# Modulation halves as products in column groups of TensorE, and second-block handovers without counters of free banks

## What is computed

```python
# first block
c_act = jax.nn.silu(c)
ada = c_act @ w_ada[l] + b_ada[l]                    # 1024 -> 6144
sh1, sc1, g1, sh2, sc2, g2 = jnp.split(ada, 6, axis=-1)
h = modulate(rmsnorm(x, norm1_g[l]), sh1, sc1)
z = h @ w_in[l]
# convolutions, RG-LRU, head norms, w_out, then a PEER expert layer
# second block
proj = rms_norm(x, w) @ w_in
# block attention on one half of the heads, gated delta rule on the other:
t_inv = lax.linalg.triangular_solve(a + eye, eye)    # 64 x 64 chunks
u = t_inv @ (v * beta); w = t_inv @ (k_beta * jnp.exp(gc))
# scan over chunks: v_new = u - w @ S; o = q @ S + intra @ v_new; S = S * g + k @ v_new
```

## Time and profile before

| | |
|---|---|
| runs | 1891.62, 1891.71, 1889.61 us (median 1891.62) |
| profiled execution | 1888.98 us, its span 1887.3 us |
| mean granted TensorE clock | 0.979 |
| TensorE busy | 1824.0 us, 97% |
| VectorE, ScalarE, GpSimd busy | 1522.8, 716.2, 1046.0 us |

### The profile page before, as it was taken

The page is one execution under the profiler, slowest core; times in us unless marked ns, Lnnn a source line. Parts: engine busy times, 40 slices in busy tenths (PEclk is TensorE's granted clock), DMA queues, the critical chain, the costliest instruction groups (busy, mean ns, idle before and its releaser), DMA issues.

```text
span 1887.3 us, 29394 instructions
## 1 busy us (share of the span) xinstructions
PE 1824.0 (97%) x10499; PEld 1599.6 (85%) x10499; DVE 1522.8 (81%) x2519; ACT 716.2 (38%) x1157; POOL 1046.0 (55%) x651
## 2 busy tenths in 40 slices
PE   8998999999999999999999999999999998999887
PEld 8877788999999999999988888888888685887666
DVE  7886888869999888888499999999998886655542
ACT  2333333333333444444333333333333434236652
POOL 1333236688888655556567767676775563345012
PEclk8998999999999999999999999999999999999999
DMA  8642343699999689988899999999997231210011
GB/s 312 215 159 81 117 138 108 206 316 317 327 321 323 227 310 312 309 308 303 314 360 359 360 357 359 355 362 356 366 356 254 72 96 60 79 45 3 2 67 46
DMA packets 159920, 440.52 MB, mean 233 GB/s; under 512 B 13648, under 2 KB 62928, under 8 KB 156752
## 3 DMA queue, kind: packets, MB, share of 16 engines
q1 hardware_dynamic: 64400, 254.71, 38.8%
q0 software_dynamic: 36864, 134.23, 18.9%
q10 hardware_dynamic: 58560, 50.34, 8.1%
HBM read 386.80 MB, written 52.43 MB: 233 GB/s over the span
## 4 chain that ended last, share of the span: by engine, by line
PE 85%; DVE 8%; ACT 2%; DMA 2%; issue 2%; ACTq 0%; SPq 0%; POOL 0%; DVEq 0%
PE PS L964 14%; PE PS L973 14%; PE PS L965 14%; PE PS L1263 9%; PE PS L1264 9%; PE PS L1272 9%; PE PS L1230 4%; PE PS L1308 2%; DVE arena L1948 2%; PE PS L991 1%; PE PS L1299 1%; PE PS L1004 1%; DVE arena L2093 1%; PE PS L999 1%; DMA xres<-in_x 1%
## 5 line engine op out<-in xcount | busy, mean ns | idle before, releaser
L852 POOL TENSOR_TENSOR w_lo<-raw,w_hi 128x1024 fp32r<-128x1024 f32 x299 | 720.2, 2410 | 727.6 <-ACT w_hi L1496 726.5
L1496 ACT ACTIVATE w_hi<-raw 128x1024 fp32r<-128x1024 f32 x332 | 351.7, 1060 | 924.2 <-PE PS L973 576.5
L964 PE MATMUL PS<-act_hi,w_hi 128*128 128x384 f32 (+1 forms) x1584 | 578.2, 365 | 6.9 <-ACT w_hi L1496 3.1
L965 PE MATMUL PS<-act_lo,w_hi 128*128 128x384 f32 (+1 forms) x1584 | 565.4, 357 | 0.0
L973 PE MATMUL PS<-act_hi,w_lo 128*128 128x384 f32 (+1 forms) x1584 | 338.6, 355 | 0.1
L964 PEld LDWEIGHTS PS<-act_hi,w_hi 128*128 128x128 f32 x1584 | 300.6, 190 | 44.1 <-issue 8.5
L965 PEld LDWEIGHTS PS<-act_lo,w_hi 128*128 128x128 f32 x1584 | 300.7, 190 | 22.2 <-issue 1.4
L973 PEld LDWEIGHTS PS<-act_hi,w_lo 128*128 128x128 f32 x1584 | 286.0, 189 | 23.8 <-issue 0.9
L1263 PE MATMUL PS<-w_hi,act_hi 128*128 128x512 f32 x768 | 299.9, 390 | 3.6 <-ACT arena L1649 3.6
L1264 PE MATMUL PS<-w_hi,act_lo 128*128 128x512 f32 x768 | 299.5, 390 | 0.0
L2317 DVE TENSOR_TENSOR act_lo<-arena,act_hi 128x384 fp32r<-128x384 f32 x128 | 249.0, 1945 | 28.6 <-ACT act_hi L1707 28.6
(11 more groups left out here) (352 smaller groups left out, 1979.6 us busy)
## 6 DMA issues: line engine op xcount, KB each, us to landing
raw<-in_expert_u SPq DMA_DIRECT2D x128, 512.0 KB, 5.9
raw<-in_expert_v SPq DMA_DIRECT2D x128, 512.0 KB, 6.4
raw<-in_w_in SPq DMA_DIRECT2D x52, 512.0 KB, 3.6
arena<-in_w_ada SPq DMA_DIRECT2D x24, 1024.0 KB, 6.8
gel_d<-arena ACTq DMA_DIRECT2D x64, 384.0 KB
gates_d<-arena ACTq DMA_DIRECT2D x12, 2048.0 KB, 15.8
arena<-gates_d SPq DMA_DIRECT2D x32, 768.0 KB, 6.9
arena<-gel_d SPq DMA_DIRECT2D x32, 768.0 KB, 8.7
```

Source lines behind the costliest of these rows:

```text
L852: pool.tensor_tensor(w_lo[:, k % SPLIT, :], raw[:, k % RAW, :], w_hi[:, k % SPLIT, :].bitcast(F32), ALU.subtract).then_inc(lo_split, 1)
L964: pe.matmul(own, w, act_hi[:, c, 0:n_tok], start=(i == 0), stop=False)
L965: pe.matmul(own, w, act_lo[:, c, 0:n_tok], start=False, stop=False)
L1496: act.activation(w_hi[:, k % SPLIT, :], raw[:, k % RAW, :], ACT.Copy).then_inc(hi_split, 1)
```

## The change

Halves 0 to 3 of the modulation are no longer summed over c on VectorE. c_tiles holds for each of the eight chunks 128 by 32 numbers, the first column cs, the others zero. ada_first(h) multiplies them with the pieces: for each of the two pieces four products of 512 columns, each into its own group of 32 partitions (and so of the array's columns) of one bank. VectorE copies that bank to acc (gathered), and ada_half sums over the partitions as before. Halves 2 and 3 have places of their own (ada_x), so their transfers wait for nothing. x comes in two parts ahead of half 0. The warm-up products go from 36 to 16. ada_first(2) stands before step 2 of the first pair and ada_first(3) before step 7. sum_ready and its waits and nops are gone; the roots wait for sq_used. bank_free is gone; wait_free waits for the counter that the reader raises anyway, and the readers' last operation raises it itself.

```diff
+        ada_x = region("ada_x", 6160, 4, 2048)
+        c_tiles = region("c_tiles", 28184, KC, 32)
...
+        def emptied(name):
+            kind, n, tb = name[0], name[1] if len(name) > 1 else 0, name[-1]
+            if kind in ("x", "xt") or (kind == "m" and n == 0):
+                return d_ready, TB + TB * n + tb + 1
+            if kind == "m":
+                return m1_ready, TB * (n - 1) + tb + 1
+            return {"ba": (ba_row, 1), "bat": (ba_sb, 1), "cum": (cum_in, 1),
+                    "gcr": (at_ready, n + 1), "br": (at_ready, n + 1), "kk": (at_ready, n + 1), "qk": (at_ready, n + 1),
+                    "kt": (tok_act, n + 1), "vt": (tok_dve, n + 1),
+                    "wt": (wu_ready, n + 1), "u": (wu_ready, n + 1), "ws": (vn_ready, n), "su": (state_ready, n + 1),
+                    "o": (o_ready, n + 1) if n < TB - 1 else (g_scaled, GH * TB),
+                    "av": (avt_ready, n + 1), "gt": (gn_done, n + 1)}[kind]
...
         def wait_free(eng, *name):
             n = JOBS[name]
             if n >= 4:
-                eng.wait_ge(bank_free[n % 4], sum(READERS[n % 4:n:4]))
+                eng.wait_ge(*emptied(NAMES[n - 4]))
...
             def ada_half(h):
-                for i in (2 * h, 2 * h + 1):
-                    if i >= 4:
-                        sp_.wait_ge(*piece_used(i - 4))
...
+                for half in range(2):
+                    piece, landed_in, _ = ada_piece(h, half)
+                    if h in (4, 5):
+                        sp_.wait_ge(ada_read, h - 3)
+                    elif h >= 6:
+                        sp_.wait_ge(ada_used, 2 * (h - 6) + half + 1)
+                    sp_.dma_start(piece, A["w_ada"][h][:, 2048 * half:2048 * half + 2048]).then_inc(landed_in, 16)
...
+            for i in range(2):
+                own = slice(4 * i, 4 * i + 4)
+                sp_.dma_start(xres[:, own, :], A["x"].rearrange("(c p) t -> p c t", p=P)[:, own, :]).then_inc(x_in[i], 16)
             ada_half(0)
-            sp_.dma_start(xres[:, :, :], A["x"].rearrange("(c p) t -> p c t", p=P)).then_inc(x_in, 16)
             ada_half(1)
...
                 mm.then_inc(sq_used, 1)
-                if c == count - 1:
-                    pe.wait_ge(sq_used, first + count)
-                    pe.nop().then_inc(sum_ready, 1)
...
+            def ada_first(h):
+                if h == 0:
+                    pe.wait_ge(c_ready, 2)
+                if h == 3:
+                    pe.wait_ge(ada_acc, 3)
+                for half in range(2):
+                    piece, landed_in, count = ada_piece(h, half)
+                    pe.wait_ge(landed_in, count)
+                    for g in range(4):
+                        mm = pe.matmul(PS[32 * g:32 * g + 32, ADA_BANK[h], :], c_tiles[:, 4 * half + g, :],
+                                       piece[:, 512 * g:512 * g + 512], start=(half == 0), stop=(half == 1),
+                                       skip_group_check=True)
+                mm.then_inc(ada_read, 1)
...
-            for n in range(36):
+            for n in range(16):
                 pe.matmul(PS[:, 7, 0:P], ones[:, :], ones[:, :], start=True, stop=True)
...
+            ada_first(0)
+            norm_back(1, 7)
+            ada_first(1)
             ada_half(0)
-            norm_back(1, 7)
             ada_half(1)
...
                 if i == 0:
-                    idle_products(12, 2)
+                    idle_products(12, 6)
+                if i == 2:
+                    ada_first(2)
+                if i == 7:
+                    ada_first(3)
...
-            weighted(0)
-            weighted(1)
+            def gathered(h):
+                dve.wait_ge(ada_read, h + 1)
+                if h >= 2:
+                    dve.wait_ge(ada_done, h - 1)
+                v.tensor_copy(acc[:, h % 2, :], PS[:, ADA_BANK[h], :]).then_inc(ada_acc, 1)
+            norm_invert(0)
+            gathered(0)
+            gathered(1)
...
-                    per_head(VB[:, tb % 2, :], ("vt", tb), beta, 4 * tb)
-                    chain.wait()
-                    freed(dve.nop(), "kt", tb)
-                    freed(dve.nop(), "vt", tb)
-                    dve.nop().then_inc(tok_dve, 1)
+                    per_head(VB[:, tb % 2, :], ("vt", tb), beta, 4 * tb, last=tok_dve)
...
-                        chain.post(v.tensor_tensor(d, d, PS[:, bank("x", n, tb), 0:256], ALU.subtract))
-                    chain.wait()
-                    if n < LEVELS - 1:
-                        freed(dve.nop(), "x", n, tb)
-                    freed(dve.nop(), "xt", n, tb)
-                    dve.nop().then_inc(d_ready, 1)
+                        v.tensor_tensor(d, d, PS[:, bank("x", n, tb), 0:256], ALU.subtract).then_inc(d_ready, 1)
```

More of the change, by code:

```diff
@@ L178, in _jobs @@
         if kind == "products":
-            job(("gcr", *n), 2)
+            job(("gcr", *n))
             job(("br", *n))
@@ L424, in build @@
         consts_in = sem("consts_in")
[L425 removed]
+        x_in = [sem(f"x_in{i}") for i in range(2)]
         ada_in = [sem(f"ada_in{i}") for i in range(4)]
+        ada_x_in = [sem(f"ada_x_in{i}") for i in range(2)]
         ada_used = sem("ada_used")
[L428 removed]
+        ada_read = sem("ada_read")
         ada_acc = sem("ada_acc")
@@ L564, in wait_free, with ada_piece @@
             if n >= 4:
-                eng.wait_ge(bank_free[n % 4], sum(READERS[n % 4:n:4]))
+                eng.wait_ge(*emptied(NAMES[n - 4]))
         def unit_bank(n):
             return n % 4 if n < 12 else n % 2 if n < 32 else (n + 1) % 2
[L571 to L575, removed]
+        def ada_piece(h, half):
+            if h in (2, 3):
+                return ada_x[:, 2 * (h - 2) + half, :], ada_x_in[h - 2], 32
+            n = 2 * (h % 2) + half
+            return ada_w[:, n, :], ada_in[n], 16 * (1 if h < 2 else (h - 4) // 2 + 2)
         def cvp(n):
@@ L1501, in square, with root @@
                 act.activation(sq[:, n % 2, :], src, ACT.Square).then_inc(sq_ready, 1)
-            def root(index, width):
-                act.wait_ge(sum_ready, index + 1)
+            def root(index, width, sums, summed):
+                act.wait_ge(sums, summed)
                 if index >= 2:
@@ L1939, in weighted @@
                     dve.wait_ge(ada_done, h - 1)
-                for c in (range(4 if h in PE_SHARE else KC) if part is None else range(4 * part, 4 * part + 4)):
-                    i = 2 * h + c // 4
+                for c in range(KC) if part is None else range(4 * part, 4 * part + 4):
+                    piece, landed_in, count = ada_piece(h, c // 4)
                     if c % 4 == 0:
-                        dve.wait_ge(ada_in[i % 4], 16 * (i // 4 + 1))
-                    w = ada_w[:, i % 4, 512 * (c % 4):512 * (c % 4) + 512]
+                        dve.wait_ge(landed_in, count)
+                    w = piece[:, 512 * (c % 4):512 * (c % 4) + 512]
                     if c == 0:
@@ L1963, in _ @@
             v.tensor_scalar(cs, cth, 0.5, None, ALU.mult).then_inc(c_ready, 1)
+            chain.link(v.memset(c_tiles[:, :, :], 0.0))
+            v.tensor_scalar(c_tiles[:, :, 0], cth, 0.5, None, ALU.mult).then_inc(c_ready, 1)
             dve.wait_ge(c_ready, 1)
@@ L2393, in per_head @@
                 for h in range(GH):
-                    chain.post(v.tensor_scalar(h4(dst)[:, h, :], PS[:, bank(*name), h * P:(h + 1) * P],
-                                               scalars[:, at + h:at + h + 1], second, *ops))
+                    ins = v.tensor_scalar(h4(dst)[:, h, :], PS[:, bank(*name), h * P:(h + 1) * P],
+                                          scalars[:, at + h:at + h + 1], second, *ops)
+                if last is not None:
+                    ins.then_inc(last, 1)
             def all_heads(ap):
@@ L2409, in _ @@
                         else:
-                            dve.wait_ge(pads_ready, 1)
+                            chain.wait()
                         v.tensor_tensor(cin[:, n % 2, 3:515], PS[:, unit_bank(n), :], rr, ALU.mult).then_inc(p_dve, 1)
```

169 lines of the change are left out of this document (48 added, 121 removed).

## The result

The changed kernel takes 1871.97 us (median of four runs, 1868.33 to 1875.54) where the kernel before took 1890.61 beside it: 0.9901 of its time, 95% interval [0.9886, 0.9915], 18.6 us less. Run twice more beside other kernels it gave 1874.36 and 1875.54 us, 0.9918 [0.9903, 0.9933] and 0.9918 [0.9902, 0.9934]. The profiled execution took 1873.56 us.

What follows compares the result with a forecast made beforehand. TensorE, busy for 97% of the span, was taken as the bound. Savings of 6.1 + 2.1 + 1.0 + 2.7 + 0.1 = 12.0 us gave a median of 1879.6 us against 1891.62, range 1876 to 1887.5.

Steps and rivals of the forecast that it cites:

- Start, -6.1: Kernel start: early x and halves on TensorE bring first normed 1.9, second 3.1 and the pair's end 1.1 us; 6.1 in all.
- a bound of 2 us on the clock: Uncertainty given to the whole sum for TensorE's clock: plus or minus 2 us.
- Sums, second block, -2.1: Second block: TensorE no longer waits for its own sum; four of eight stalls count, 0.53 us each, 2.1 us saved.
- Sums, first block, -1.0: First block: nine head and token sums have such a stall, most beside VectorE; 1.0 us saved.
- Handovers, -2.7: Chain from 1698 to 1786: some twelve handovers shorter by 0.1 to 0.3 us without counters and nops; 2.7 us saved.
- The bound that I set: Handover saving lies between nothing and the 3.9 us of issue in the chain 1752 to 1786 and the like before it.
- Two groups at a time: In ada_first only two column groups run together, 3.6 us per half; total -6.4 us, 1885.2 us; chance 0.24.
- One after the other: In ada_first the column groups run serially, 6.9 us per half; total +7.2 us, 1898.8 us, slower; chance 0.06.
- Lead lost: Start's gain vanishes through a 1.2 GHz clock or unchanged later times; only 5.9 us remain, 1885.7 us; chance 0.10.
- waits do not go: Stalls behind sums and readers' waits stay as long, so only the start counts; 1885.5 us; chance 0.05.
- 1.3 us for the halves: Uncertainty of the sum for ada_first at the start, if a half takes 1.7 us: -1.3 us.

Runs made afterwards that it cites:

- the part alone: Kernel before with only the new start: halves 0 to 3 in column groups, x in two parts ahead, 16 warm-up products; 0.9978, 4.2 us less.
- sums alone: Kernel before with only the counter of finished sums and its waits and nops removed; 0.9968 of the kernel before, 6.0 us less.
- the parts: Kernel before with one part each: new start, 4.2 us less; no counter of finished sums, 6.0; no counters of free banks, 6.6.
- the full-width products: Changed kernel with each of the 32 products of ada_first at full width, so none runs beside another; 1892.68 us, 1.0008 of the kernel before.
- the order of transfers alone: Kernel before with x in two parts ahead of half 0 and 16 warm-up products, all halves still on VectorE; 1.0012 of the kernel before.

## Why the prediction was right or wrong

**Start, -6.1.** The mechanism and its times are confirmed step by step: sums over at 18.76 (forecast 18.9), half 0 at 22.3 (22.9), first normed 28.68 (28.9), second 44.50 (44.5), the pair's end 5.7 us earlier (6.1). I had chosen 2.0 us per half from rows with two groups; it is 1.85. The scaled figure of the Trainium skill (TensorE: Matmul & The Clock Gate, Part 3), an estimate of 2.2 us, was on the high side: the ratio measured is 3.7, not 3.2. But this is the better of two starts. Of the seven profiled executions with this start three have the first normed at 28.7 to 29.0 and four at 31.1 to 31.8. In two other executions of the changed kernel the lead at the gates is 2.7 and 3.2 us. The third one's chain:

```profile
4.22 6.24 PE PS L1080 x32
10.46 11.30 PE PS L1011 x64
21.76 3.57 PE PS L1066 x16
25.33 1.05 PE PS L1019 x4
26.38 1.85 PE PS L1066 x16
```

The warm-up products take 6.24 and not 5.26 us (I had 4.8): TensorE passes 12 records per microsecond from 8 us on in the first and only from 10 us on in the third. Then the clock falls for the sums sooner, between 12 and 13 and not at 14 us, and they take 11.3 and not 9.3. With 16 warm-up products their end varies from 9.5 to 11.0 between executions, with 36 it was 14.7 to 15.3, beside x at 14.5. That the shorter warm-up brought this into play is argued from these times; no run changed it alone. My sum had it only as a bound of 2 us on the clock. So the forecast of this term was right for one outcome and some 3 us too good for the other; the part alone gave 4.2 us over eleven runs.

**Sums, second block, -2.1: too small.** The price per stall was right (0.50 for 0.53). Two steps failed. I counted four stalls of 0.53; by the chains of the two kernels five count, at 0.50, 0.47, 1.16, 0.52 and 0.66 us. The one at 1617 is among them. Its row named ScalarE's w_hi as the releaser, but with sums alone the same product (L963, the second row) starts before that operation ends at 1615.68, so it does not need that tile:

```profile
1614.62 1.06 ACT L1481 ACTIVATE w_hi<-raw 128x1024 fp32r<-128x1024 f32 x1 [4.19 <-PE PS L972]
1614.80 0.80 PE L963 MATMUL PS<-act_hi,w_hi 128*128 128x512 f32 x1
```

The releaser is inferred, and what the unit waited for was the sum. And where a stall falls into a stretch at 1.2 GHz it costs more, and it makes the stretch later: over the unit behind the sum at 1600 the kernel with sums alone saves 1.16 us. Over the eight sums that kernel gained 3.3 us, the changed kernel 3.5, 4.2 and 4.2.

**Sums, first block, -1.0: too small.** I took most of the nine stalls to be beside VectorE. From the gates to 269 us the lead grows by 2.4 us in each of the three executions of the changed kernel and by 2.1 with sums alone, and by nothing in the kernels that keep the wait. How these 2.4 us divide between stalls and clock is not settled. Between 110 and 260 us the kernel before has four stretches at the low clock, from 146, 166, 180 and 248 us; in the changed kernel the one at 180 is absent, with sums alone those at 146 and 248.

**Handovers, -2.7: too small.** Measured 4.3 to 4.8, of which 3.3 to 3.6 are idle time of TensorE and the rest its busy time. The step that failed first is the price of a handover: I counted those that the chain shows as issue, at 0.1 to 0.3 us. A reader's wait, its nops and the counter are in series, and two engines hand over to each other, so one link of the chain gained 0.72 and the next 0.55; some of that stood in the chain as queue steps of VectorE and ScalarE and not as issue. The second is a term that I put at nothing: shorter waits also spared a drop of the clock, 0.8 to 1.6 us of busy time. The bound that I set was counted in issue alone and did not hold this term.

**Rivals.** Two groups at a time: excluded by 1.85 us and by four passes under way at once. One after the other: did not happen, but its price was right, shown by the full-width products (its 4.1 for each us per half was a little high: its own terms, 19.2 us for 4.9, give 3.9). Lead lost, waits do not go: excluded by the parts. None of them covers what happened. The step of the prediction that failed is the worth of the removed waits and counters: 2.1 + 1.0 + 2.7 = 5.8 us in the sum, 6.0 + 6.6 = 12.6 us as measured alone, while the start was put too high (6.1, measured 4.2). That bound was missing in the range: below 1876.0 it had only 1.3 us for the halves and 2 for the clock, and none for the count and price of the waits.

## What to carry to other kernels

A matrix-vector product with long rows is worth putting into column groups: four products with 32 columns each ran together here and cost about a quarter of the full-width form (1.85 for 6.87 us). When a wait on the busiest engine goes, count with what the clock gives back too: behind waits of 2.7 to 4.1 us TensorE ran its next 4 to 7 us at 1.2 GHz, so by an estimate from these windows a microsecond of waiting cost up to two. And where such a wait can't go, fill it with idle products into a bank that is free by then: 47 short ones gave 9 us here, over half the gain of the whole change, for a few lines. Moving a stage forward can also make it collide with another engine's work, as the order of transfers alone did.

## What was not expected of the hardware

- TensorE's clock fell here though the engine was busy: in the sums at the start, products of one column, TensorE is busy in each microsecond from 5 us on, and the granted clock is 0.50 from 14 us (or 13). One or two idle products of 128 columns between the sums did not hold it: it was 0.50 from 16 us.
- At the very start the granted clock of the rows reads 1.00 while TensorE passes 7 records per microsecond, and 12 later at the same reading; the rate of the products tells more there than the clock's column.
- A VectorE operation with two operands in memory took 2.73 us in place of 0.76 beside a GpSimd operation of 2.5 us.
